# Moving the lower parts of six gate pieces of mixer 2 from GpSimd to VectorE

## The reference, cut to what matters

```
z = h @ w_in
u_val, u_gate, q, k, v, f_logit, gate_c, gate_a = jnp.split(z, offs, axis=-1)
conv_out = conv_module(u_val, u_gate, ...)          # 31 taps per channel, layer norm, silu, projection
attn_out = forgetting_attention(q, k, v, ...) @ w_attn_out[l]   # 8 heads, softmax over masked scores
mixed = jax.nn.sigmoid(gate_c) * conv_out + jax.nn.sigmoid(gate_a) * attn_out
x = x + g1 * (mixed @ w_out[l])
```

## Time and profile before

| | |
|---|---|
| median of 3 runs | 1820.61 us (1818.64 to 1821.32) |
| profiled execution | 1821.09 us |
| its span, first to last instruction | 1819.2 us |
| TensorE busy | 1750.2 us, 96% |
| VectorE, ScalarE, GpSimd busy | 947.7, 537.4, 837.1 us |
| mean granted TensorE clock | 0.995 of full speed |

### The profile page before, as it was taken

The page is one execution under the profiler, slowest core; times in us unless marked ns, Lnnn a source line. Parts: engine busy times, 40 slices in busy tenths (PEclk is TensorE's granted clock), DMA queues, the critical chain, the costliest instruction groups (busy, mean ns, idle before and its releaser), DMA issues.

```text
span 1819.2 us, 29474 instructions
## 1 busy us (share of the span) xinstructions
PE 1750.2 (96%) x10938; PEld 1109.0 (61%) x10939; DVE 947.7 (52%) x1423; ACT 537.4 (30%) x857; POOL 837.1 (46%) x491
## 2 busy tenths in 40 slices
PE   8999999999899999999999999999999999999997
PEld 8999896889899988888433333333333333333332
DVE  7776643466776766846642333444434433343344
ACT  6443444655644454463210110101101011011011
POOL 0000001000000038556477777777777767777774
PEclk9999999999999999999999999999999999999999
DMA  9777443235485634327999999999999999999994
GB/s 380 270 261 268 169 179 110 76 116 197 177 284 198 211 116 167 129 106 279 369 429 429 428 428 429 428 428 428 429 428 428 429 371 420 427 429 428 429 428 197
DMA packets 55262, 560.96 MB, mean 308 GB/s; under 512 B 6208, under 2 KB 7360, under 8 KB 14400
## 3 DMA queue, kind: packets, MB, share of 16 engines
q1 hardware_dynamic: 54912, 560.03, 76.8%
q10 hardware_dynamic: 288, 0.07, 0.0%
HBM read 559.03 MB, written 1.05 MB: 308 GB/s over the span
## 4 chain that ended last, share of the span: by engine, by line
PE 59%; DMA 23%; issue 6%; POOL 5%; ACT 4%; DVE 3%; SPq 0%; POOLq 0%; DVEq 0%; ACTq 0%
DMA stage<-w_exp_in 22%; PE bank L726 11%; PE bank L728 11%; PE bank L727 11%; PE bank L1326 10%; PE bank L1415 5%; POOL ring L1916 4%; PE bank L1338 2%; PE bank L1304 2%; DMA ring<-stream 1%; PE bank L704 1%; ACT w_hi L1475 1%; PE bank L853 1%; DVE arena L1941 1%; PE bank L1316 1%
## 5 line engine op out<-in xcount | busy, mean ns | idle before, releaser
L1916 POOL COPY ring<-stage 128x2048 f32<-128x2048 f32 x372 | 693.7, 1894 | 254.8 <-DMA stage<-w_exp_in 100.8
L1326 PE MATMUL bank<-ring,arena 128*64 128x512 f32 x2112 | 476.3, 597 | 18.0 <-POOL ring L1916 17.3
L726 PE MATMUL bank<-x_hi,w_hi 128*128 128x256 f32 (+1 forms) x1336 | 384.5, 288 | 17.4 <-DVE x_lo L1941 4.4
L728 PE MATMUL bank<-x_hi,w_lo 128*128 128x256 f32 (+1 forms) x1336 | 380.0, 284 | 0.0
L727 PE MATMUL bank<-x_lo,w_hi 128*128 128x256 f32 (+1 forms) x1336 | 379.7, 284 | 0.0
L1326 PEld LDWEIGHTS bank<-ring,arena 128*64 128x64 f32 x2112 | 141.3, 136 | 317.0 <-issue 228.8
L1896 POOL TENSOR_TENSOR w_lo<-ring,w_hi 128x512 fp32r<-128x512 f32 x104 | 134.9, 1329 | 402.8 <-ACT w_hi L1475 402.8
L726 PEld LDWEIGHTS bank<-x_hi,w_hi 128*128 128x128 f32 x1336 | 253.3, 190 | 24.8 <-issue 11.6
L1960 DVE TENSOR_TENSOR w_lo<-ring,w_hi 128x2048 fp32r<-128x2048 f32 x91 | 208.1, 2287 | 99.5 <-ACT w_hi L1475 99.3
L728 PEld LDWEIGHTS bank<-x_hi,w_lo 128*128 128x128 f32 x1336 | 253.5, 190 | 0.0
L727 PEld LDWEIGHTS bank<-x_lo,w_hi 128*128 128x128 f32 x1336 | 252.8, 189 | 0.2
(11 more groups left out here) (374 smaller groups left out, 2004.7 us busy)
## 6 DMA issues: line engine op xcount, KB each, us to landing
stage<-w_exp_in SPq DMA_DIRECT2D x124, 2048.0 KB, 10.5
stage<-w_exp_out SPq DMA_DIRECT2D x62, 2048.0 KB, 10.6
ring<-stream SPq DMA_DIRECT2D x119, 1024.0 KB, 4.9
arena<-ada SPq DMA_DIRECT2D x48, 512.0 KB, 5.0
ring<-w_exp_in SPq DMA_DIRECT2D x8, 1024.0 KB, 8.7
ring<-w_exp_out SPq DMA_DIRECT2D x4, 1024.0 KB, 13.7
cst<-const_in SPq DMA_DIRECT2D x1, 1608.0 KB, 20.9
arena<-b_exp SPq DMA_DIRECT2D x3, 384.0 KB, 9.4
```

What stands on the lines that cost most here:

```text
L726: begin = mm(out_, wh, xh, start=start, stop=False)
L728: return begin, mm(out_, wl, xh, start=False, stop=stop)
L1326: last = mm(bank[2 + gu][pr, :], xT[:, k % 4, k // 4, :], ring[:, k, c0:c0 + 512], start=False, stop=(k == KD - 1), tile_position=pos)
L1916: nc.gpsimd.tensor_copy(ring[:, j, :], stage[:, 2 * PAIR_PLACE[j // 2 % 3] + j % 2, :]).then_inc(in_place, 1)
```

## The change

The six gate pieces 12 to 17 of mixer 2 are taken out of GpSimd's list and put into VectorE's. VectorE makes the lower part of piece 12 + h in head h (h from 0 to 5), behind fa_max(h + 1) and ahead of the convolution taps, with `rest`: a wait for w_high of the piece, then one instruction of 128 x 2048. TensorE waits for w_lower in place of w_split for these pieces; since VectorE's pieces are no longer the first ones of the stream without a gap, they get an order of their own. Gate pieces 10 and 11 and all others of mixer 2 stay with GpSimd.

```diff
-POOL_PIECES = [p for p in SPLIT_PIECES if p >= MIX2_AT]
-DVE_PIECES = [p for p in SPLIT_PIECES if p < MIX2_AT]
+MIX2_GATES = range(MIX2_AT + 12, MIX2_AT + 18)
+POOL_PIECES = [p for p in SPLIT_PIECES if p >= MIX2_AT and p not in MIX2_GATES]
+DVE_PIECES = [p for p in SPLIT_PIECES if p < MIX2_AT or p in MIX2_GATES]
+DVE_ORDER = {p: n for n, p in enumerate(DVE_PIECES)}
 POOL_ORDER = {p: n for n, p in enumerate(POOL_PIECES)}
...
                         if p in POOL_ORDER:
                             pe.wait_ge(w_split, (POOL_ORDER[p] + 1) * RESTS)
                         elif p in ORDER:
-                            pe.wait_ge(w_lower, ORDER[p] + 1)
+                            pe.wait_ge(w_lower, DVE_ORDER[p] + 1)
...
                 soft_norm("fa", h, p2, P)
                 if h + 1 < HEADS:
                     fa_max(h + 1)
+                if h < len(MIX2_GATES):
+                    rest(MIX2_GATES[h])
                 conv_taps(TAPS_PER_HEAD if h < LN_HEAD - 1 else len(taps))
```

## The result

The changed kernel took 1828.62 us, median of 7 runs (1824.36 to 1829.46), against 1820.45 us (7 runs, 1816.55 to 1821.85) for the one before: ratio 1.0042, 95% interval 1.0031 to 1.0054. It is 8.2 us slower. Its profiled execution took 1828.89 us with a span of 1827.1 us, 7.9 us over the span before.

The account below looks back on a forecast made before the run. TensorE alone was taken to set the pace, with VectorE taking over in heads 0 to 3. 8.4 us of delay plus 1.3 for the clock gave 9.7, so 1830.3 us against the median; range 1824.5 to 1833.8.

Parts of the forecast that it names:

- The main step: Mixer 2, heads 0 to 3: VectorE, waiting some 2.8 us per head for w_high, sets the pace; TensorE loses 8.38 us.
- VectorE's cycle: Reciprocal to reciprocal in the heads: reduces, wait, lower part and taps sum to 11.79 us, then 11.01 and 6.31.
- The run of the heads: From head 0's reciprocal to head 5's transposes on TensorE; delay of 7.33 + 0.35 + 0.70 = 8.38 us forecast.
- the clock, 1.3 us: Granted clock falls behind the last late head, at 784.9 to 788.9 us: 1.3 us lost, bounds 0 and 2.8.
- the fall behind the last gap isn't covered: Clock fall after the gap at 781.11 us: 2.6 us lie behind the last wait at 786.33, so 1.3 us is lost.
- the three waits of the forecast: TensorE's transposes wait on VectorE in heads 2, 3 and 4 by 1.3, 2.4 and 1.6 us.
- The end: Everything after the heads hangs on TensorE, so 8.4 + 1.3 = 9.7 us goes through to the end in full.
- The cover that holds: Heads: w_high is ready when VectorE asks, cycle 8.97 us, no change, time 1820.6 us; chance 0.08.
- Part of the delay lost at the wait on o_lo: Behind the last head: the 2.7 us wait absorbs delay, leaving 5.7 us, time 1826.3 us; chance 0.08.
- The clock making TensorE the slow engine again: Clock falls in every one of the heads: 13.2 us at most, time 1833.8 us; chance 0.09.
- The freed port as a gain: Behind the last head: without GpSimd beside o_lo's lowering, TensorE's 2.7 us wait could go, time 1817.9 us; chance 0.03.

Follow-up runs that it names:

- experiment 1: Changed kernel with the six lower parts on VectorE asked for behind the taps of each head, not ahead: 1818.5 us, ratio 0.9993 to the kernel before.
- experiment 5: Changed kernel with ScalarE making the upper part of piece 12 + h ahead of exp_fa(h + 1) in heads 0 to 5: 1820.71 us, ratio 0.9997 to before.
- experiment 2: Kernel before, GpSimd making all lower parts, with only VectorE's wait for w_high put ahead of the taps in heads 0 to 5: 1820.75 us, ratio 0.9999.
- experiment 3: The change for pieces 12 to 14 only (heads 0 to 2), the others left on GpSimd: 1828.2 us, ratio 1.0041 to the kernel before.
- experiment 4: The change for pieces 15 to 17 only (heads 3 to 5), pieces 12 to 14 left on GpSimd: 1819.64 us, ratio 0.9993 to the kernel before.
- experiment 6: Kernel before with piece 19's upper part behind ScalarE's conversion of the convolution's rows: 1814.50 us, ratio 0.997; with its lower part also on VectorE: 1813.84 us, 0.9966.

## Why the prediction came out as it did

**The main step was right, and right in its parts.** The forecast was 9.7 us (1830.3 us), the measurement 8.2 us (1828.62 us). VectorE's cycle was worked out at 11.79, 11.01 and 6.31 us and measured at 11.75, 10.96 and 6.26; the wait at 2.82 and measured 2.78. "VectorE becomes what sets the pace" is what the chain shows: it goes through VectorE and ScalarE from head 0 to head 4. The run of the heads was to grow by 8.38 us and grew by 8.27. Experiments 1 and 5 show that the wait is the cause, experiment 2 that it needs the work beside it, experiments 3 and 4 how the lead of the first heads is used up. That the medians also differ by 8.2 is in part luck: the 8.38 was worked out from a profile with the short low clock in head 0, and against one with the longer stretch the same cycles of VectorE cost 6.7 us. How many of the timed runs are of which kind isn't known.

**The term that was mis-sized is the clock, 1.3 us; the profile shows nothing of it.** I put a fall of the clock behind the last late head, where nothing would hide it. In the profile it came earlier: low from 733.9 to 740.4, 2.5 us longer than before, and from 771.3 to 778.9. The first took up the lead that I had counted as a wait in head 2 (forecast 1.3 us, measured none), the second the wait in head 4 (forecast 1.6, measured none); only head 3 waited, 2.25 us for 2.35. Behind head 3 TensorE stood idle only once more, for 0.27 us at 785.34, and behind head 4 the clock stayed at 1.00 up to the wait on o_lo. TensorE reached the transposes of head 4 some 0.4 us behind VectorE's rows, and its next wait, for the evacuation, took that up again (785.34 us, where the forecast less the 0.72 us of the start gives 785.61). The step that failed is "the fall behind the last gap isn't covered": the gap of 1.57 us that it was to follow had become one of 0.27. One profile shows this; that it is so in every run isn't shown. So the three waits of the forecast were wrong one by one, while their sum was right: in a stretch whose pace another engine sets, a slower TensorE only turns idle time into busy time.

**The end.** That the delay goes through to the end in full held for the 8.27: the first projection was as late as the transposes of head 5. The small gains and losses behind it (0.95 back, 1.3 more) are not the change's.

**The rivals.** The cover that holds is what experiment 5 built, and experiment 1 by asking later, at the ratio that the rival had named (no change); so its deciding point, whether w_high is there when VectorE asks, was the right one. Part of the delay lost at the wait on o_lo: no, that wait is 2.7 us in both profiles; its chain moved along with TensorE. The clock making TensorE the slow engine again: it fell twice in the heads and not in every one, and the most that it set was 0.4 us at head 4, given back at the next wait. The freed port as a gain: it is real on VectorE (0.55 for 2.39 us), and experiment 1, which has it without the wait, is at 0.9983 to 1.0002; a gain up to 0.17% isn't excluded, a large one is.

**The shared port.** The scalings took 2.39 us beside GpSimd's piece and 0.55 without it, the lowerings of o_hi 5.27 and 1.43, the taps 5.58 and 5.57. "SBUF — State Buffer" of the Trainium skill, section "SBUF: two separate sides", says that a port pair is shared by GpSimd and by those VectorE instructions that have two inputs in SBUF or run in a mode that uses two ports, and that whoever is first holds it for a whole instruction. The lowerings, with two inputs, agree with it; for the scalings, with one, no run shows the mode. The time that VectorE gets back was worth nothing that can be told in the heads, where TensorE doesn't wait for it. At the lowerings TensorE does wait, and there it is a part, not measured by itself, of the 5.5 us of experiment 6.

## What to carry to other kernels

Before work is moved to a faster engine, look not at its duration but at who releases it, and at what stands behind it in that engine's order: an engine that is idle half of the span can still be full in the stretch in question. Here the releaser was itself waiting for the engine that asked, so that every head paid the way there and back on VectorE; asking one block of work later made the same move free. And look for the place where the bounding engine waits at all: of the seven pieces that these runs moved about, only the one ahead of such a wait was worth anything.

## What the runs showed that I had not expected

The low clock comes at the same places but lasts differently from run to run. Ahead of the heads, behind the same gap of 1.2 us, it was low for 4.0 us in the kernel before and for 6.5 us in the changed one, and behind the wait on o_lo for 5.6 and 3.2 us. Behind a wait near 836 us, which all kernels with ScalarE's old order at piece 19 have (1.5 us and then 0.8 us), it fell in three of the profiles (experiments 2, 3 and 5: for some 4 us between 838 and 846 us) and not in the others. At half the clock, 2 us more or less of such a stretch is 1 us of TensorE's time, and the fastest and slowest runs of one kernel here are 3.5 to 8 us apart. The loop over the experts adds its own: from SyncE's issue to the end it took 959.6 us before, 960.9 in the changed kernel, 958.2 in experiment 1 and 961.1 in experiment 3, with nothing changed in it. What decides either isn't shown by these runs.
